# Sums over partitions as split products with ones, the head sums half a tile later, and query norms with the data as moving operand

## The reference, cut to what matters

```python
def retention_layer(x, ...):                  # layer 1, 4 heads, dk 256, dv 512
    h = rmsnorm(x, norm_w) @ w_in             # q | k | v | gate, 6144 columns
    q, k = rotary(q), rotary(k) * dk ** -0.5
    S, o = retention(q, k, v, S0)             # decayed causal, with a state per head
    o = rmsnorm(o, gn_w)                      # per head: mean of squares over dv = 512
    return x + (o * silu(g)) @ w_out, S
k, v = split(rmsnorm(x, kv_norm_w) @ w_kv)    # shared keys and values, k normed per head
def moba(x, ...):                             # layer 2, 8 heads of 128
    q, g = split(rmsnorm(x, norm_w) @ w_in)   # mean of squares over 1024
    q = rmsnorm(q, q_norm_w) * hd ** -0.5     # per head: mean of squares over 128
    return x + (attend(q, k, v) * silu(g)) @ w_out
```

## Time and profile before

| | us |
|---|---|
| median of three runs | 511.89 |
| lowest, highest | 511.84, 512.19 |
| the profiled execution, time | 513.17 |
| the profiled execution, span from first to last instruction | 511.4 |
| TensorE busy (share) | 504.7 (99%) |
| VectorE busy | 350.7 (69%) |
| ScalarE busy | 262.1 (51%) |
| GpSimd busy | 74.3 (15%) |
| DMA read and written | 98.93 MB, 27.57 MB |
| granted TensorE clock | 1.000 of full |

### The profile page before, as it was taken

One profiled execution on the slowest core, in us unless ns is written; L12 is line 12 of the kernel. 1 busy time (PEld: TensorE's weight loads), 2 busy tenths in 40 slices (PEclk: granted clock), 3 DMA queues, 4 the chain that ended last, 5 costly groups with the idle time before them and its releaser, 6 DMA issues.

```text
span 511.4 us, 9183 instructions
## 1 busy us (share of the span) xinstructions
PE 504.7 (99%) x3410; PEld 436.0 (85%) x3410; DVE 350.7 (69%) x647; ACT 262.1 (51%) x532; POOL 74.3 (15%) x85
## 2 busy tenths in 40 slices
PE   8999999999999999999999999999999999999997
PEld 6989978899779978897898999987777778999885
DVE  3855539883889729893598967745756664676662
ACT  5835532573438633563652545764444645655640
POOL 0291005420082003620000240000000000000000
PEclk9999999999999999999999999999999999999999
DMA  9993969999799998999937976526697647784211
GB/s 283 306 345 116 276 240 331 373 350 242 280 347 372 227 271 305 360 315 203 264 110 273 342 227 249 185 84 215 235 344 231 232 154 235 237 306 163 82 53 51
DMA packets 79231, 125.49 MB, mean 245 GB/s; under 512 B 3907, under 2 KB 42004, under 8 KB 79060
## 3 DMA queue, kind: packets, MB, share of 16 engines
q1 hardware_dynamic: 79106, 124.89, 75.9%
q10 hardware_dynamic: 82, 0.02, 0.0%
HBM read 98.93 MB, written 27.57 MB: 247 GB/s over the span
## 4 chain that ended last, share of the span: by engine, by line
PE 84%; DVE 7%; DMA 3%; ACT 2%; SPq 1%; issue 1%; POOL 0%; DVEq 0%; ACTq 0%; POOLq 0%
PE bank L875 40%; PE bank L872 17%; PE bank L857 6%; PE bank L1045 3%; DMA w_raw<-in_ret_w_out 3%; PE bank L990 2%; DVE w_lo L1520 2%; PE bank L1058 2%; PE bank L1112 1%; PE bank L1004 1%; PE bank L937 1%; DVE st L1736 1%; PE bank L1158 1%; PE bank L891 1%; PE bank L1145 1%
## 5 line engine op out<-in xcount | busy, mean ns | idle before, releaser
L1520 DVE TENSOR_TENSOR w_lo<-w_raw,w_hi 128x512 fp32r<-128x512 f32 x207 | 144.9, 738 | 70.8 <-ACT w_hi L1182 70.2
L1182 ACT ACTIVATE w_hi<-w_raw 128x512 fp32r<-128x512 f32 x208 | 118.5, 620 | 59.0 <-PE bank L875 33.8
L875 PE MATMUL bank<-xn_hi,w_hi 128*128 128x320 f32 x320 | 100.4, 318 | 0.6 <-ACT w_hi L1182 0.6
L875 PE MATMUL bank<-xn_hi,w_lo 128*128 128x320 f32 x320 | 97.6, 309 | 0.0
L875 PE MATMUL bank<-xn_lo,w_hi 128*128 128x320 f32 x320 | 97.5, 309 | 0.0
L872 PE MATMUL bank<-w_hi,xn_hi 128*128 128x512 f32 x160 | 65.0, 406 | 0.0
L875 PEld LDWEIGHTS bank<-xn_hi,w_hi 128*128 128x128 f32 x320 | 59.7, 188 | 4.9 <-issue 3.2
L872 PE MATMUL bank<-w_lo,xn_hi 128*128 128x512 f32 x160 | 62.6, 391 | 0.0
L872 PE MATMUL bank<-w_hi,xn_lo 128*128 128x512 f32 x160 | 62.5, 390 | 0.0
L875 PE MATMUL bank<-ym_hi,w_hi 128*128 128x320 f32 x192 | 61.4, 320 | 0.0
L875 PEld LDWEIGHTS bank<-xn_lo,w_hi 128*128 128x128 f32 x320 | 59.8, 188 | 0.3
(11 more groups left out here) (259 smaller groups left out, 752.2 us busy)
## 6 DMA issues: line engine op xcount, KB each, us to landing
w_raw<-in_ret_w_in SPq DMA_DIRECT2D x23, 1024.0 KB, 11.2
st<-in_state_ret SPq DMA_DIRECT2D x32, 512.0 KB, 8.6
out_ret_state_sample<-st SPq DMA_DIRECT2D x32, 512.0 KB, 4.5
w_raw<-in_ret_w_out SPq DMA_DIRECT2D x8, 1024.0 KB, 9.1
w_raw<-in_moba_w_in SPq DMA_DIRECT2D x8, 1024.0 KB, 6.2
cache<-in_cache_k SPq DMA_DIRECT2D x16, 512.0 KB, 4.9
w_raw<-in_w_kv SPq DMA_DIRECT2D x8, 1024.0 KB, 6.0
cache<-in_cache_v SPq DMA_DIRECT2D x16, 512.0 KB, 4.1
```

Of the source, the lines that this page charges most:

```text
L875: mm = pe.matmul(bank[out][:, 0:T], w[:, wk, P * tile:P * tile + P], x[:, k, :], **flags)
L1182: act.activation(w_hi[:, c % 2, part], w_raw[:, c % RAW, part], ACT.Copy).then_inc(w_hi_done, 1)
L1520: dve.tensor_tensor(w_lo[:, c % 2, part], w_raw[:, c % RAW, part], w_hi[:, c % 2, part].bitcast(F32), ALU.subtract).then_inc(w_lo_done, 1)
```

## The change

All sums over partitions that were fp32 products with `ones` become two split products. A new step `SP` stands right behind `GNA`: ACT rounds the sum in `scr[:, 4]` to fp32r (`sums_hi`), and DVE subtracts it from the sum (`sums_lo`). `SS` multiplies both by `ones_r`, an fp32r copy of ones which ACT makes once, in the first step `SP`. In the loops, `SS` moves from the end of the second `rv` tile to the middle of the third; in `ro` it moves from slot 6 to slot 8 (two slots are one tile), `SR` from 8 to 9, `SM` from 9 to 10 and `SH` from 11 to 12. The three `NS` products become one pair, at the middle of the first `mq` tile; DVE adds the last two squares itself (`NA`, in two parts), and ACT and DVE split that sum too. In `QS` the four products with one moving column become four with the squares as moving operand (128 columns) and 32 stationary columns of `pick`, each to its own 32 partitions; their result is turned by a third transpose in `QT`, and root and reciprocal move there. The masks `own` are loaded by a DMA of their own at chunk 3.

The diff (left out: names of tiles and semaphores, the entries of `SP` and `NA` in the table of banks):

```diff
@@ -190,7 +190,7 @@
             fill(7, "OSM")
-        if s == ("NS", 5):
+        if s == ("NS",):
             fill(5, "NORM", 1)
@@ -198,7 +198,7 @@
         return [[], [("XC", h, 0), ("XC", h, 1), ("UP", h, 0)], [("UP", h, 1)], [("UP", h, 2)], [("UP", h, 3)], [],
-                [("FX", h), ("GNA", h), ("SG", h)], [("US", h)], [("SS", h)], [("SR", h), ("SM", h)]]
+                [("FX", h), ("GNA", h), ("SP", h), ("SG", h)], [("US", h)], [], ([("SS", h)], [("SR", h), ("SM", h)])]

@@ -217,22 +217,21 @@
     g = [[] for _ in range(32)]
-    for at, step in ((0, ("XC", 3, 0)), (0, ("XC", 3, 1)), (1, ("SH", 2)), (4, ("FX", 3)), (4, ("GNA", 3)), (5, ("SG", 3)),
-                     (6, ("SS", 3)), (8, ("SR", 3)), (9, ("SM", 3)), (11, ("SH", 3)), (13, ("UP", 3, 0)), (16, ("UP", 3, 1)),
+    for at, step in ((0, ("XC", 3, 0)), (0, ("XC", 3, 1)), (1, ("SH", 2)), (4, ("FX", 3)), (4, ("GNA", 3)), (4, ("SP", 3)), (5, ("SG", 3)),
+                     (8, ("SS", 3)), (9, ("SR", 3)), (10, ("SM", 3)), (12, ("SH", 3)), (13, ("UP", 3, 0)), (16, ("UP", 3, 1)),
                      (19, ("UP", 3, 2)), (22, ("UP", 3, 3)), (24, ("US", 3))):
...
         g[18 + 2 * n] += [("SQ", n), ("W", n)]
-        if n == 5:
-            g[20 + 2 * n].append(("NS", n))
-    g[31].append(("NS", KT - 2))
+    g[31].append(("NA", 0))
     g[29].append(("MB",))
...
     add("SQ", KT - 1)
-    mid = [[("NS", KT - 1)]] + [[("ME", n)] + ([("QS", 0)] if n == 5 else []) for n in range(MH - 1)]
+    add("NA", 1)
+    mid = [[("NS",)]] + [[("ME", n)] + ([("QS", 0)] if n == 5 else []) for n in range(MH - 1)]
     end = [[("RMS",)]] + [[] for _ in range(MH - 1)]
@@ -317,8 +316,13 @@
         scr_split = sb("scr_split", [P, KT * T], F32R)
-        eye = sb("eye", [P, 2 * P + 4])
-        ident, ones, own = eye[:, 0:P], eye[:, P:2 * P], eye[:, 2 * P:2 * P + 4]
+        eye = sb("eye", [P, P + 4])
+        plain = ExitStack()
+        ones = sb("ones", [P, P], F32, plain)
+        plain.close()
+        ones_r = sb("ones_r", [P, P], F32R)
+        sums_hi, sums_lo = (scr_split[:, n * T:n * T + T] for n in (5, 6))
+        ident, own = eye[:, 0:P], eye[:, P:P + 4]
         wcols = sb("wcols", [P, 48])
@@ -408,7 +412,7 @@
         sqs = flat_sqs.rearrange("p (g h m) -> p g h m", g=2, m=32)
-        q_rows = mvp[:, 1, 0:TP]
+        q_rows = mvp[:, 1, 0:TP + P]
         ops = ps.ap().rearrange("p s t -> p (s t)")[:, 0:4 * P]
@@ -678,7 +683,7 @@
             sp.wait_ge(first_w_loaded, 16)
-            sp.dma_start(eye[:, P:2 * P + 4], a["c_eye"][:, P:2 * P + 4]).then_inc(ones_loaded, 16)
+            sp.dma_start(ones[:, :], a["c_eye"][:, P:2 * P]).then_inc(ones_loaded, 16)
             load_chunk(1)
@@ -695,6 +700,7 @@
                             .then_inc(pages_loaded, 16)
+                        sp.dma_start(own, a["c_eye"][:, 2 * P:2 * P + 4]).then_inc(own_loaded, 16)
                     if 6 <= c < 10:
@@ -907,15 +913,10 @@
                 elif kind == "NS":
-                    kt = step[1]
-                    if kt == KT - 3:
-                        await_free(pe, 5, "NORM", 1)
-                        pe.wait_ge(pair_sum_done, 5)
-                    else:
-                        pe.wait_ge(sq_done, RH + kt + 1)
-                    mm = pe.matmul(bank[5][:, 0:T], ones, scr[:, kt, :], start=kt == KT - 3, stop=kt == KT - 1)
-                    if kt == KT - 1:
-                        close(mm, 5)
+                    pe.wait_ge(sum_lo_done, RH + 1)
+                    await_free(pe, 5, "NORM", 1)
+                    pe.matmul(bank[5][:, 0:T], ones_r[:, :], sums_hi, start=True, stop=False)
+                    close(pe.matmul(bank[5][:, 0:T], ones_r[:, :], sums_lo, start=False, stop=True), 5)
                 elif kind == "MM":
@@ -1008,9 +1009,10 @@
                 elif kind == "SS":
-                    pe.wait_ge(sq_sum_done, step[1] + 1)
+                    pe.wait_ge(sum_lo_done, step[1] + 1)
                     await_free(pe, 5, *step)
-                    close(pe.matmul(bank[5][:, 0:T], ones, scr[:, 4, :], start=True, stop=True), 5)
+                    pe.matmul(bank[5][:, 0:T], ones_r[:, :], sums_hi, start=True, stop=False)
+                    close(pe.matmul(bank[5][:, 0:T], ones_r[:, :], sums_lo, start=False, stop=True), 5)
                 elif kind == "BT":
@@ -1026,13 +1028,13 @@
                         for pair in range(4):
-                            mm = pe.matmul(bank[5][:, TP + pair:TP + pair + 1], flat_sqs[:, P * pair:P * pair + P], ones[:, 0:1],
+                            mm = pe.matmul(bank[5][32 * pair:32 * pair + 32, TP:TP + P], pick[:, 1:33], flat_sqs[:, P * pair:P * pair + P],
                                            start=True, stop=True)
...
                     await_free(pe, 7, *step)
-                    for t in range(2):
+                    for t in range(3):
                         mm = pe.transpose(bank[7][:, P * t:P * t + P], q_rows[:, P * t:P * t + P], ident)
@@ -1418,6 +1420,16 @@
                     act.activation(scr[:, 4:8, :], scr[:, 0:4, :], ACT.Square).then_inc(sq_done, 1)
+                elif kind == "SP":
+                    h = step[1]
+                    if h == 0:
+                        act.wait_ge(ones_loaded, 16)
+                        act.activation(ones_r[:, :], ones[:, :], ACT.Copy)
+                    act.wait_ge(sq_sum_done, h + 1)
+                    act.activation(sums_hi, scr[:, 4, :], ACT.Copy).then_inc(sum_hi_done, 1)
+                elif kind == "NA" and step[1] == 1:
+                    act.wait_ge(sq_sum_done, RH + 1)
+                    act.activation(sums_hi, scr[:, 7, :], ACT.Copy).then_inc(sum_hi_done, 1)
                 elif kind == "SS":
@@ -1433,14 +1445,15 @@
                     await_full(act, 5, "QSS")
-                    act.activation(rsq[:, 16:20], bank[5][:, TP:TP + 4], ACT.Sqrt, bias=eps[:, 1:2])
-                    act.activation(q_rows, bank[5][:, 0:TP], ACT.Copy).then_inc(bank_read[5], 1)
+                    act.activation(q_rows, bank[5][:, 0:TP + P], ACT.Copy).then_inc(bank_read[5], 1)
                 elif kind == "QT":
...
                     for t in range(2):
-                        ins = act.activation(roots[:, t], bank[7][:, P * t:P * t + P].rearrange("p (j m) -> p j m", m=32)[:, :, 0:2],
-                                             ACT.Sqrt, bias=eps[:, 1:2])
+                        act.activation(roots[:, t], bank[7][:, P * t:P * t + P].rearrange("p (j m) -> p j m", m=32)[:, :, 0:2],
+                                       ACT.Sqrt, bias=eps[:, 1:2])
+                    ins = act.activation(rsq[:, 16:20], bank[7][:, TP:TP + P].rearrange("p (j m) -> p j m", m=32)[:, :, 0],
+                                         ACT.Sqrt, bias=eps[:, 1:2])
                     ins.then_inc(bank_read[7], 1)
@@ -1751,6 +1764,19 @@
                     dve.tensor_tensor(scr[:, 4, :], scr[:, 4, :], scr[:, 5, :], ALU.add).then_inc(sq_sum_done, 1)
+                elif kind == "SP":
+                    dve.wait_ge(sum_hi_done, step[1] + 1)
+                    dve.tensor_tensor(sums_lo, scr[:, 4, :], sums_hi.bitcast(F32), ALU.subtract).then_inc(sum_lo_done, 1)
+                elif kind == "NA" and step[1] == 0:
+                    dve.wait_ge(pair_sum_done, 5)
+                    dve.wait_ge(sq_done, RH + KT - 1)
+                    done(dve.tensor_tensor(scr[:, 6, :], scr[:, 6, :], scr[:, 5, :], ALU.add))
+                elif kind == "NA":
+                    done.wait()
+                    dve.wait_ge(sq_done, RH + KT)
+                    dve.tensor_tensor(scr[:, 7, :], scr[:, 7, :], scr[:, 6, :], ALU.add).then_inc(sq_sum_done, 1)
+                    dve.wait_ge(sum_hi_done, RH + 1)
+                    dve.tensor_tensor(sums_lo, scr[:, 7, :], sums_hi.bitcast(F32), ALU.subtract).then_inc(sum_lo_done, 1)
                 elif kind == "SG":
@@ -1782,13 +1808,9 @@
                     dve.tensor_copy(line[:, 0:FAR + 1], bank[6][0:MH, 0:FAR + 1]).then_inc(bank_read[6], 1)
-                elif kind == "QR":
-                    await_read(dve, 5, "QSS")
-                    done(dve.reciprocal(rsq[:, 16:20], rsq[:, 16:20]))
-                    done.wait()
                 elif kind == "QT":
                     await_read(dve, 7, *step)
-                    done(dve.reciprocal(rsq[:, 0:16], rsq[:, 0:16]))
+                    done(dve.reciprocal(rsq[:, :], rsq[:, :]))
                     done.wait()
@@ -1957,7 +1979,7 @@
                     pool.wait_ge(bias_loaded, 16 * MH)
-                    pool.wait_ge(ones_loaded, 16)
+                    pool.wait_ge(own_loaded, 16)
                     done.wait()
...
                         at = TS // 2 * (u // 2)

```

(5 more changed lines are left out.)

## The result

| | median, us | lowest to highest | runs |
|---|---|---|---|
| before | 512.19 | 511.84 to 514.39 | 5 |
| changed | 515.45 | 514.25 to 515.51 | 5 |

The ratio is 1.0057, with a 95% interval of 1.0043 to 1.0071: 2.2 to 3.6 us slower. A second set of runs of the same kernel gave 1.0066 (1.0050 to 1.0082). Forecast were 514.7 and +2.8. The profiled executions are closer together than the medians, 514.71 (span 512.9) against 513.17 (span 511.4): that of before was one of its slower ones, that of the changed kernel one of its faster.

A forecast was written before the change was run, and what follows sets the result against it. The prediction took PE, busy 99% of the span, as the bound. Terms 0.4 + 1.2 + 1.2 + 0.3 + 0.4 - 0.5 gave +3.0, taken as +2.8: median 514.7 us, own range 513.2 to 516.5.

The forecast's parts named there:

- DVE's detour of 1.0 and `rg`: SP delays DVE's `w_lo` parts by 1.0, making PE later at `rg` by 0.1, 1.0 and 1.0 us in loops 1-3.
- OP, 0.7 in all: Delayed ACT and DVE work makes `vp_lo` late for PE at OP: 0.3, 0.2 and 0.2 us in loops 1-3.
- The fourth sum, +0.3: In `ro`, the stall and saving (1.2 + 0.25) are given back as a new wait on `w_lo` part 2: +0.3 us.
- Norm, +0.4: Before `mq`, a wait of 1.6, the pair and refill cost 2.0 against the three products' 1.6: +0.4 us.
- QS and QT, -0.5: Four products with M = 32 save 0.73 and the third transpose costs 0.24: net 0.5 us saved.
- The clock: Rival: five new waits drop PE to 1.2 GHz for one tile each, 18 us, giving 529; chance 0.03.
- rival 2: SyncE's queue: late weight load moves DVE's chain at `ro` by 2.0, not 0.6; +1.4 more, 516.1 and above; chance 0.06.
- Covers held: Rival: idle time on ACT and DVE hides the added work, no new waits; -4.0, 507.9 us; chance 0.12.

The follow-up runs named there:

- `dummy_q`: The kernel before with QS and QT changed, plus two unread 128x320 subtractions on DVE behind the sum of squares in the three loops: 514.04 us.
- `lo_last`: The changed kernel with PE's wait on `vp_lo` moved behind OP's other waits and first two products: 515.34 us.
- `fourth_only`: The kernel before with only the fourth head's sum split and moved; loops, norm and QS as before: 512.59 us.
- `q_only`: The kernel before with only the change of QS and QT, all sums over partitions as before: 511.36 us.
- `norm_only`: The kernel before with only the norm sum split: 512.88 us.
- `norm_end`: The changed kernel with NS at the end of the first `mq` tile instead of its middle: 516.43 us.
- `dve_rounds`: The changed kernel with the high part of the four head sums rounded on DVE instead of ACT: 512.95 us.
- `q_again`: `q_only` run once more, unedited, as the base for other runs on the same chip: 511.43 us.

## Why the forecast came out right, and where it was wrong

**DVE's detour of 1.0 and `rg`: right.** L1786 starts 1.00 behind the sum, and `dummy_q` shows that the 1.0 is paid whole in the second and third loop. The first trace shows 0.4 instead; the faster pair of `w_lo` parts beside GpSimd goes with it.

**OP, 0.7 in all: wrong, 2.1 to 2.5.** The step "ready at 230.4, PE there at 230.2: another 0.2" had the lateness of the operand about right. `vp_lo` ends at 231.65 in the trace, 3.27 later than before, with PE 2.30 later and 0.84 of slack in the earlier trace rows: 0.13 late. (Counted from the loop's FX, `vp_lo` is 1.41 and PE 0.45 later in the first trace and 1.95 and 0.94 in the second, for the forecast 2.0 and 1.0.) What failed is that a wait was priced at the lateness of its operand. PE restarts 0.47 to 0.50 behind it, three times, and has its usual spacing again 0.08 later; `lo_last` takes this restart away, but gets back only 1.0 to 1.2 of the 2.1 to 2.4, since SF then waits.

**The fourth sum, +0.3: wrong in its size.** The step "0.8 late at most, 0 if the DMA is short of bandwidth; I take 0.6" failed. The landing came 1.29 and 0.85 earlier relative to PE, not 0.6 later, so the new wait was 0 and 0.16 instead of 1.5. And the stall of 1.2 that the earlier trace rows gave was the far end of what executions show. Against the median, `fourth_only` is +0.4 (-0.2 to +0.9), which holds the forecast: less of a stall to win, less of a new wait. The load was indeed issued 0.3 to 0.9 later against PE in the seven traces in which the loops made PE late. But it took 12.3 to 13.3 us to land there (12.8 on average), and 13.1 to 14.6 (13.8) in the seven others, that of before among them: on average the landing did not follow the issue. Why it took less is not shown, and in a single trace the scatter, 1.41 between before and `q_only`, is as large as the effect.

**Norm, +0.4: right in size**, shown by `norm_only`, with the wait of 1.4 for the forecast 1.6. The reason was incomplete. The earlier trace rows were read as PE's time against one operand; but `norm_end` shows that PE's time there is worth little, since the chain of DVE and ACT behind the sum holds PE at the latest when `mk` starts. In the changed trace its `w_lo` part is done 0.24 before PE uses it, so PE could win back that much and no more. And the chain itself is 0.4 late: L1625, the reciprocal behind the sum, starts at 309.27 for 307.22 before, 2.05 later, with PE 1.64 later ahead of the norm. The lines, PE behind DVE:

```profile
307.54 0.49 DVE L1779 TENSOR_TENSOR scr_split<-scr,scr_split 128x320 fp32r<-128x320 f32 x1 [0.54 <-ACT scr_split L1432]
...
308.08 0.41 PE L918 MATMUL bank<-scr_split,ones_r 128*128 128x320 f32 x1 [1.44 <-DVE scr_split L1779]
```

**QS and QT, -0.5: right.** -0.57 in each trace. In the chain the four products of M = 32 take 0.22 where the earlier trace rows have 0.98. Three transposes take 0.33, where two took 0.22 before, so the third costs 0.11 and not 0.24:

```profile
343.67 0.22 PE bank L1031 x8
...
345.94 0.33 PE bank L1038 x3
```

The two transposes in the chain of before:

```profile
344.57 0.22 PE bank L1036 x2
```

**Rivals.** The clock stayed at its upper level (2.4 GHz): the mean granted over the span was 0.999 or 1.0 in every profiled execution, with up to eight waits of 0.15 us and more behind the first 90 us. One timed run of `fourth_only` had a mean of 0.948 and took 513.48; another with 1.0 took the same, and no trace shows what happened in it. SyncE's queue came 0.3 to 0.9 late against PE, but no landing was later against PE than that of before, where rival 2 wanted 0.8. Covers held at one place, the fourth sum, and only in some executions.

**The sum.** The 2.8 came out by luck, because errors of both signs met: in the first trace OP +1.4, `rg` -1.05, the fourth sum -1.6. The last of these is largely the late landing in the one trace of before. Against `q_only`, whose old sum had no wait, the first trace of the changed kernel is 3.3 longer and the second 4.3, and so 2.8 and 3.8 with the 0.5 of QS and QT taken off, around the 2.9 and 3.4 of the medians; there the errors of the first are OP +1.4, `rg` -1.2 and the fourth sum -0.5. The parts alone add up to +4.6 (4.3 + 0.4 + 0.7 - 0.8), the whole is 2.9 and 3.4. Each part's interval is 0.6 or 0.7 to either side, 1.3 together, so this gap can be noise; it isn't explained.

## What to carry over

Two tests show whether work can be taken from the busiest engine for a price on another. First find the stretches where the helper has no slack before its next consumer: there each microsecond put into DVE cost PE one in the second and third loop, whatever PE saved. Then look at every engine that the new step makes wait, with its queue: here ACT's wait, at OP, cost 2.1 to 2.5 us where DVE's work, at `rg`, cost 1.1 to 2.3, and doing both halves on one engine gave most of it back. And a stall, or a landing, read from one execution is one draw: compare several before pricing a gain by it.

## What the runs showed of the hardware

- From the end of the awaited operand to PE's product it was 0.47 to 0.50 us at OP, where three more waits, already satisfied, stand behind the one for `vp_lo` (twelve cases in four traces), and 0.26 at SF in `lo_last`. At `rg`, where none stands behind, it was 0.14 to 0.15, but at NS, with one behind, 0.05. So the place in the queue matters at OP, where `lo_last` varied it, but the number of waits behind is not the whole rule.
- GpSimd at work beside DVE changes DVE's times. A copy of 128x320 from fp32 to fp32r took 0.33 alone (third loop of `dve_rounds`) and 0.88 in the second loop, where GpSimd's last rotary step ran from 153.99 for 1.12. DVE, then GpSimd:

```profile
154.41 0.88 DVE L1820 CAST scr_split<-scr 128x320 fp32r<-128x320 f32 x1
155.33 0.49 DVE L1822 TENSOR_TENSOR scr_split<-scr,scr_split 128x320 fp32r<-128x320 f32 x1
```

```profile
153.99 1.12 POOL L2006 TENSOR_TENSOR kT<-raw_qk 128x320 f32<-128x320 f32 x1
```

The copy ends 0.18 behind GpSimd's step, as if its start had been put off until that step's end. The Trainium skill, page "SBUF — State Buffer", section "SBUF: two separate sides", says that the two engines share one pair of ports, and that an instruction of either that needs the pair (on DVE one with two inputs in SBUF, or one in a two-port mode) holds it to its end. The trace agrees: the same two `w_lo` parts took 1.29 with GpSimd idle and 1.96 to 2.67 beside it.
- The same 1 MB load, issued at 231.02 and 231.06 in two programs that differ up to there by two small loads, was used 1.5 us apart. In two executions of one program (`q_only` and `q_again`; no edit lies between them) it was used at 244.83 and 245.07, 0.24 apart, and over all fourteen traces it took 12.3 to 14.6 us from issue to landing.
